# Moving a token's 1/rms from in front of the last feed-forward's input projection to behind it

## The reference

```python
x = x + merged @ w_out[l]                  # output projection, 1024 -> 1024
h = rmsnorm_2(x, norm_ffn[l])              # x * rsqrt(mean(x*x) + eps) * g, per token
ug = causal_dwconv(h @ w_ffn_in[l], conv_w[l], conv_b[l])   # 1024 -> 2 x 2816, 3 taps along the tokens
u, g = jnp.split(ug, 2, axis=-1)
x = x + (jax.nn.silu(g) * u) @ w_ffn_out[l]                 # 2816 -> 1024
return rmsnorm_2(x, norm_final)
```

## Time and profile before

| | |
|---|---|
| median of 3 runs | 2339.95 us (2339.5 to 2340.85) |
| the profiled execution | 2344.62 us, its span 2342.8 us |
| PE busy | 2249.7 us, 96% of the span |
| DVE, ACT, POOL busy | 1229.7, 964.7, 929.5 us |
| last product of `w_out` starts | 1946.29 us into the span |
| first product of `g_out` starts | 2206.39 us |
| mean granted TensorE clock | 0.971 of full |

### The profile page before, as it was taken

How to read it: one execution, slowest core, us unless ns; L and a number is a source line. 1 busy time by engine, 2 the same in 40 slices (tenths; PEclk the granted TensorE clock), 3 DMA queues, 4 the chain that set the end, 5 groups by cost and what they waited for, 6 DMA issues and landing times.

```text
span 2342.8 us, 29281 instructions
## 1 busy us (share of the span) xinstructions
PE 2249.7 (96%) x10522; PEld 1782.9 (76%) x10522; DVE 1229.7 (52%) x1714; ACT 964.7 (41%) x1398; POOL 929.5 (40%) x386
## 2 busy tenths in 40 slices
PE   6999999999979999989999999989999898999998
PEld 4788788788867777767788888878777687888886
DVE  6776665521287787786422221330777744555412
ACT  4224433233435546544433333443555624444332
POOL 1444344346614334324244446535222142444463
PEclk8999899999989999999899999999999999999999
DMA  7553465553315344332223223334221131332232
GB/s 298 180 217 126 143 247 211 179 149 93 111 42 183 108 140 149 110 113 84 67 94 95 93 69 98 102 97 136 93 74 46 32 104 56 108 97 91 76 92 73
DMA packets 74097, 273.84 MB, mean 117 GB/s; under 512 B 8519, under 2 KB 11207, under 8 KB 67736
## 3 DMA queue, kind: packets, MB, share of 16 engines
q1 hardware_dynamic: 70632, 266.74, 34.6%
q10 hardware_dynamic: 3376, 5.90, 0.8%
HBM read 269.21 MB, written 8.12 MB: 118 GB/s over the span
## 4 chain that ended last, share of the span: by engine, by line
issue 60%; POOL 24%; PE 15%; POOLq 1%; DVE 0%; ACT 0%; DVEq 0%
POOL wlo L500 24%; PE bank L522 15%; POOLq L499 0%; POOLq L502 0%; DVE y L2003 0%; PE bank L578 0%; POOLq L500 0%; PE bank L570 0%; DVE x L1996 0%; DVEq L123 0%; ACT sq L1018 0%; ACT root L1000 0%; DVE root L1436 0%; DVEq L2001 0%; POOLq L2131 0%
## 5 line engine op out<-in xcount | busy, mean ns | idle before, releaser
L500 POOL TENSOR_TENSOR wlo<-raw,whi 128x1024 fp32r<-128x1024 f32 x382 | 929.3, 2437 | 1388.2 <-ACT whi L989 1387.5
L522 PE MATMUL bank<-h_hi,whi 128*128 128x512 f32 x1584 | 641.6, 405 | 25.4 <-POOL wlo L500 20.0
L522 PE MATMUL bank<-h_hi,wlo 128*128 128x512 f32 x1584 | 629.9, 398 | 0.0
L522 PE MATMUL bank<-h_lo,whi 128*128 128x512 f32 x1584 | 628.9, 397 | 0.0
L989 ACT ACTIVATE whi<-raw 128x1024 fp32r<-128x1024 f32 x382 | 401.1, 1054 | 548.4 <-PE bank L522 517.7
L522 PEld LDWEIGHTS bank<-h_hi,whi 128*128 128x128 f32 x1584 | 300.9, 190 | 100.8 <-issue 21.8
L522 PEld LDWEIGHTS bank<-h_hi,wlo 128*128 128x128 f32 x1584 | 300.8, 190 | 76.3
L522 PEld LDWEIGHTS bank<-h_lo,whi 128*128 128x128 f32 x1584 | 301.3, 190 | 69.7
L522 PE MATMUL bank<-g_hi,whi 128*128 128x512 f32 x592 | 235.4, 398 | 0.0
L522 PE MATMUL bank<-g_lo,whi 128*128 128x512 f32 x592 | 233.3, 394 | 0.0
L522 PE MATMUL bank<-g_hi,wlo 128*128 128x512 f32 x592 | 232.9, 393 | 0.0
(11 more groups left out here) (329 smaller groups left out, 2995.0 us busy)
## 6 DMA issues: line engine op xcount, KB each, us to landing
raw<-f_in_d SPq DMA_DIRECT2D x88, 512.0 KB, 3.5
raw<-m_d SPq DMA_DIRECT2D x65, 512.0 KB, 3.7
ada_f<-ada_d SPq DMA_DIRECT2D x24, 1024.0 KB, 5.8
raw<-g_in_d SPq DMA_DIRECT2D x44, 512.0 KB, 3.5
raw<-w_in_d SPq DMA_DIRECT2D x41, 512.0 KB, 3.5
csb<-cs_d SPq DMA_DIRECT2D x32, 640.0 KB, 6.4
ada_a<-ada_d SPq DMA_DIRECT2D x16, 1024.0 KB, 4.9
raw<-a_in_d SPq DMA_DIRECT2D x24, 512.0 KB, 6.0
```

The lines of the kernel that those rows point to most:

```text
L500: nc.gpsimd.tensor_tensor(wlo[:, s], raw[:, s], whi[:, s].bitcast(F32), ALU.subtract).then_inc(lo_ready, 1)
L522: mm = nc.tensor.matmul(psum[bank][:], w[:, s, kk, :], xs[part == "lo"][:, k, :], start=first and kk == 0 and i == 0, stop=last and kk == ...
```

## The change

The norm's gain stays in front of the projection; the factor 1/rms goes behind it.

- During `w_out` ACT makes `h_hi` and `tb` of each new `x` tile directly (gain only), DVE makes `h_lo`.
- PE takes `g_in` tile 0, then the token sums, tile 1, then the spread, then the rest, each tile alone (`single`); only tile 0 waits for `h_hi`/`h_lo` k by k (`in_ready`).
- DVE copies the spread factors from bank 4 into `rstd`. In the loop each output tile is first multiplied by `rstd` into bank 6 (value) or 7 (gate), which frees the projection's bank; the three taps read bank 6 or 7 and count up a new semaphore, `conv_out`, for which ACT's Silu waits.

```diff
@@ PE
-            def x_root(i):
+            def x_total(i):
                 pe.wait_ge(acc_x, 6 * (i + 1))
                 token_sums(4, acc[:], True)
                 pe.wait_ge(x2_out, KD * (i + 1))
                 token_sums(4, sq[:, 1, :], False).then_inc(s_done, 1)
-                spread(4, X_ROOT[i], R1)
...
-            x_root(0)
-            four("g_in", 5)
+            single("g_in", 0)
+            x_total(0)
+            single("g_in", 1, wait=False)
+            spread(4, X_ROOT[0], R1)
+            for u in range(2, 4):
+                single("g_in", u, wait=False)
             with pe.Fori(0, 10) as it:
                 for u in range(4, 8):
                     single("g_in", u, it, 4, wait=False)
@@ ACT
             for m in range(KD):
                 split_hi(C0["w_out"] + m + RING)
                 read_out(T0["w_out"] + m)
+                if m >= 2:
+
+                    act.wait_ge(in_ready, I0["g_in"] + m - 1)
+                nc.scalar.activation(h_hi[:, m, :], x[:, m, :], ACT.Identity, bias=zcol[:], scale=V("norm_ffn", m))
+                nc.scalar.activation(tb[:, m % 2, :], x[:, m, :], ACT.Identity, bias=zcol[:], scale=V("norm_ffn", m)).then_inc(in_hi, 1)
                 x_square(0, m)
...
             x_root(0)
-            plain_norm(5, "g_in", "norm_ffn")
             with act.Fori(0, 11) as it:
...
-                    read_out(t + 1, it, 4)
+                    act.wait_ge(conv_out, it * 4 + (2 * j + 2))
@@ DVE
                 TT(x[:, m, :], x[:, m, :], psum[b][:], ALU.add).then_inc(bank_free[b], 1)
+                lo_part(h_lo[:, m, :], tb[:, m % 2, :], h_hi[:, m, :], I0["g_in"] + m)
                 x_sum(0, m)
-            x_norm(0, 5, "g_in")
+            inverse(X_ROOT[0], R1)
+            dve.wait_ge(rb_done, X_ROOT[0] + 1)
+            step(nc.vector.tensor_copy(rstd[:], psum[4][:]))
...
-                        taps(buf[:, j, :], psum[t % 4][:], "g_conv", it * 2 + (KF * i + j), 3, bank_free[t % 4])
+                        TT(psum[6 + i][:], psum[t % 4][:], rstd[:], ALU.mult).then_inc(bank_free[t % 4], 1)
+                        read_out(t, it, 4)
+                        taps(buf[:, j, :], psum[6 + i][:], "g_conv", it * 2 + (KF * i + j), 3, conv_out)
```

More of the change, by code:

```diff
@@ L243, in program @@
         dve_step = sem("dve_step")
-        gate_out, prod_out = sem("gate_out"), sem("prod_out")
+        gate_out, prod_out, conv_out = sem("gate_out"), sem("prod_out"), sem("conv_out")
         dt_lin, dt_exp, a_exp, cs_ready, cs_out, tokT_done, tok_ready = (
@@ L975, in _ @@
                 down("g_out", it, (g_hi, g_lo))
-            x_root(1)
+            x_total(1)
+            spread(4, X_ROOT[1], R1)
         @block.scalar
@@ L1510, in x_sum @@
                     TT(acc[:], acc[:], sq[:, m % 2, :], ALU.add).then_inc(acc_x, 1)
[L1512 to L1520, removed]
             def mod_evac(d, it=0):
```

## The result

| | before | after |
|---|---|---|
| median | 2339.95 us (5 runs, 2339.27 to 2344.69) | 2327.8 us (5 runs, 2327.08 to 2330.16) |
| profiled execution, its span | 2344.62, 2342.8 us | 2329.19, 2327.2 us |
| last product of `w_out` issued | 1946.52 us | 1941.18 us |
| from there to the first product of `g_out` | 259.87 us | 249.08 us |
| mean granted clock | 0.971 | 0.975 |

The ratio is 0.9948, 95% interval 0.9937 to 0.996: 12.2 us less, the interval 9.4 to 14.7. Direction and mechanism came as forecast.

The account below looks back on a forecast made before the run. PE, busy 96% of the span, was taken as the bound: 13.5 us of overhead between `w_out` and `g_out`, less 3.3 kept, gives 10.2 off 2339.95, so 2329.8 us. The 8-in-10 range was 2328.3 to 2333.5.

Parts of the forecast that it names:

- what PE keeps: Between `w_out` and `g_out`: token sums, spread and slow restarts of dense products remain on PE, together 3.3 of 13.5 us.
- the two returns: On PE, going back from short to dense products after the token sums and after the spread: estimated 0.1 us each.
- Inputs of tile 0: At the start of `g_in`: `h_lo` 7 is ready at 1950.8 us, 0.6 us before PE asks, so no wait.
- DVE in the loop: In `g_in`'s loop: with the new product DVE needs 21.4 us per four tiles, staying under PE's 22.4.
- banks and the 14 us at `g_out`: If DVE lags in `g_in`: free PSUM banks and `g_out`'s late need of the last `g_lo` absorb about 7 us.
- the ring: Slots for `g_in`'s input chunks, split by ACT and POOL: released one by one, 5.6 us apart, with 7 us spare.
- The rival of a lagging DVE: In `g_in`'s loop: a 1.2 us product puts DVE 1.05 us a turn over PE; about 2334 to 2338 us, chance 0.06.
- The clock rival: Behind token sums, perhaps the spread: clock falls, costing 1.65 or 3.3 us; 2331.4 to 2333.1, chance 0.15 including tile 0 waiting.

Follow-up runs that it names:

- null runs: The kernel before and the changed kernel, each measured again unchanged: medians 2339.68 us (ratio 0.9998) and 2331.3 us (ratio 0.9953).
- mul_half: Changed kernel with the product by `rstd` done twice for the gate tiles only, one tile in two: median 2333.32 us, ratio 0.9971.
- mul_twice: Changed kernel with the product by `rstd` done twice for every output tile: median 2349.49 us, ratio 1.0038.
- sums_thrice: Changed kernel with the eight one-column token-sum matmuls repeated twice more behind the real ones, results unused: median 2335.09 us, ratio 0.9973.

## Why the prediction was right, and where it was wrong

- **The mechanism held.** PE was the bound, the seam was the only place that changed, and what was given back is what the earlier trace rows showed as waits and slow clock: PE's four waits in the seam before make 6.2 us (0.94, 0.57, 1.79, 2.88), and the other 4.6 of the 10.8 us stand beside the low clock and the sums' and spread's overhead; no run separates these. PE now has no idle time from `w_out` to `g_out`, and the granted clock is 1.00.
- **The step that failed is the sum's "what PE keeps".** The sum took 2.0 us for the token sums, 1.1 for the spread and 0.1 each for the two returns, 3.3 in all. Measured: 1.70, 0.80, and about 0.2 for the rest: 249.08 - 246.4 = 2.7. Durations of a group of matmuls were added, although the groups overlap; start to start is the cost. The gain in the seam is 10.8 us instead of 10.2.
- **The range took too little of the scatter.** Its low end left 1.5 us below the forecast for everything. The same code ahead of the seam takes up to 8 us more or less, and single executions of the changed kernel run from 2327.08 to 2332.76. Its ten timed executions have a median of 2329.0, the 62 of the kernel before 2340.2: 11.2 less, near the seam's 10.8, and 2329.0 lies inside the range. The median of the five runs in the table above lay 1.2 us below that of the ten: which five executions one gets was luck. That the rest of the 12.2 us is scatter follows from the two null runs; it was not otherwise shown.
- **Inputs of tile 0.** Right: `h_lo` 7 ended 0.54 us behind POOL (forecast 0.55) in 1.59 us (about 1.5), before PE came to k = 7 at 1941.18 + 4.90 = 1946.08, 0.54 us later (0.6).
- **DVE in the loop.** Right: a turn of 21.39 us (21.4), a product of 0.693 us in the mean of 44 (0.69). `g_lo` ran free of POOL, 0.693 us in the mean of 21; the last of the 22 starts behind this window. These are the groups of DVE after from 1941 to 2196 us, shapes kept apart, which answer to the earlier trace rows; the last figures are the idle time ahead and what ended it:

```profile
L1988 DVE TENSOR_TENSOR bank<-bank,rstd 128x512 f32<-128x512 f32 x44 | 30.5, 693 | 5.5 <-PE bank L522 5.3 <-DVE rstd L1979 0.2
...
L1439 DVE TENSOR_TENSOR g_lo<-ta,g_hi 128x512 f32 x21 | 14.6, 693 | 19.5 <-ACT g_hi L1413 19.5
```

- **What a late DVE would cost.** Wrong, without bearing on the forecast: "banks and the 14 us at `g_out`" absorb nothing. mul_half's 5 us came back as 4.66 in `g_out`, mul_twice's 21 as 22.4, both by way of the ring and not of the banks. The rival of a lagging DVE, priced at 2334 to 2338 with 7 us absorbed, would have come to 2341 to 2345.
- **The clock rival** was rightly kept a chance: the mechanism exists (sums_thrice), at about the price given (1.56 us measured, 1.65 forecast).
- **The end of the kernel** gave back 0.6 us that nobody forecast: from the final token sums to the span's end 13.8 us against 13.2. The same sums and spread stand there in either kernel, and the second group of sums lasted 1.42 us after and 1.05 before, since the clock was lower. This is scatter too: in the null runs the order is the other way round, 12.7 us with the change and 13.4 without.
- The text before the forecast gives the profiled execution as 2.0 us longer than its span; by its own numbers it is 1.8. Nothing hangs on it.

## What to carry over

A factor that belongs to a token can go behind a projection, and then the reductions that make it can be set behind full tiles of dense work: first look how long PE stands still or runs at the low clock there, since that is all there is to win. What such a move adds is an instruction per output tile on the engine that reads the tiles; work out that engine's period against PE's, and count every us beyond it in full, also where the stage itself looks unharmed. A change of half a per cent needs the seam of two traces and several executions of each kernel: the total of one trace each here was off by 5 us.

## What the hardware showed

- TensorE's clock fell behind short products without any idle gap: behind 5.3 us of one-column products (sums_thrice, to 0.51 of full, the level of 1.2 GHz, price 1.6 us, one trace), not behind 1.7 us of them (after and four more traces).
- The same code has 102 to 116 us of low clock ahead of the end of `w_out` from one execution to the next, and comes there up to 8 us later (correlation 0.94 over twelve traces).
- A DVE tap with one SBUF input, 0.49 us alone, was held to 2.08 us by POOL's subtraction, and one with two took 2.65 instead of 0.75; the same taps from PSUM ran at 0.75 beside POOL.
- A product that reads one PSUM bank and writes another takes 0.69 us for 128 x 512, as the addition from PSUM into SBUF does.
